# Expert stage in four slots by 32 tokens, with four value gathers and then four key gathers in a row

## The reference, cut to what matters

```
def peer_ffn(xn, w_q, keys1, keys2, u, v):
    q = (xt @ w_q).reshape(n, PEER_HEADS, 2, PEER_HALF)          # 8 heads, 2 x 128
    s1 = einsum('nhd,hkd->nhk', q[:, :, 0], keys1)               # 128 scores
    s2 = einsum('nhd,hkd->nhk', q[:, :, 1], keys2)
    v1, i1 = top_k(s1, 16); v2, i2 = top_k(s2, 16)
    cand = v1[..., :, None] + v2[..., None, :]                   # 256 sums
    top_s, sel = top_k(cand, 16)
    idx = take(i1 * 128 + i2, sel)                               # 16 experts per token and head
    g = softmax(top_s)
    act = gelu(einsum('pd,ped->pe', xb, u[idx]))                 # dot products of 1024
    return einsum('pe,ped->pd', g * act, v[idx])                 # weighted sum of rows of 1024
```

## Time and profile before

| | us |
|---|---|
| median of 3 runs | 4652.41 |
| lowest and highest | 4647.03, 4680.39 |
| span of the profiled execution | 4664.4 |
| expert stage in it, first gather issued to the end | 1476.6 to 4664.4 |

### The profile page before, as it was taken

The page is one execution under the profiler, slowest core; times in us unless marked ns, Lnnn a source line. Parts: engine busy times, 40 slices in busy tenths (PEclk is TensorE's granted clock), DMA queues, the critical chain, the costliest instruction groups (busy, mean ns, idle before and its releaser), DMA issues.

```text
span 4664.4 us, 46976 instructions
## 1 busy us (share of the span) xinstructions
PE 3850.8 (83%) x13480; PEld 2174.6 (47%) x13480; DVE 2478.5 (53%) x6136; ACT 1078.6 (23%) x2482; POOL 2471.3 (53%) x2212
## 2 busy tenths in 40 slices
PE   8999997899884878787887787787788787878787
PEld 7888885555442334343343343343334343434332
DVE  3111004655434666666666666666666666666665
ACT  4221113333210212212222212222222121212221
POOL 0000000000002777777777777777777777777766
PEclk9999997999967999898999898989898999898989
DMA  3222214221136999999999999999999999999988
GB/s 135 89 85 99 77 41 155 75 65 46 53 100 252 369 379 350 385 368 362 368 375 371 367 382 363 360 373 361 358 389 352 363 374 364 346 374 358 361 322 309
DMA packets 393667, 1291.38 MB, mean 277 GB/s; under 512 B 48440, under 2 KB 84536, under 8 KB 391368
## 3 DMA queue, kind: packets, MB, share of 16 engines
q0 software_dynamic: 313920, 1143.22, 65.1%
q1 hardware_dynamic: 61080, 116.93, 7.4%
q10 hardware_dynamic: 18432, 28.42, 1.7%
HBM read 1243.87 MB, written 45.71 MB: 276 GB/s over the span
## 4 chain that ended last, share of the span: by engine, by line
PE 30%; DVE 14%; DMA 12%; issue 8%; POOL 3%; ACT 2%; POOLq 0%; ACTq 0%; DVEq 0%; SPq 0%
PE e_o_ps L1776 24%; DMA e_u_rows<-in_u,e_expert 8%; PE e_q_ps L1744 4%; DMA e_v_rows<-in_v,e_expert 3%; POOL e_v_rows L1429 2%; POOL e_u_rows L1429 1%; DVE e_pairs L1583 1%; DVE e_pairs L1608 1%; DVE e_top_idx L1585 1%; DVE e_top_idx L1582 1%; DVE e_pairs L1612 1%; DVE e_picked L1614 1%; DVE e_top_val L1584 1%; DVE e_pos L1585 1%; PE e_w_ps L1731 1%
## 5 line engine op out<-in xcount | busy, mean ns | idle before, releaser
L1776 PE MATMUL e_o_ps<-e_v_rows,e_diag 128*128 128x512 f32 (+1 forms) x4352 | 2061.4, 626 | 380.7 <-ACT e_diag L1499 289.3
L1631 DVE CUSTOM_DVE_ANT_0 e_u_rows<-e_u_rows,e_xn 128x1024 f32<-128x1024 f32 x1088 | 1300.6, 1223 | 1058.0 <-DMA e_u_rows<-in_u,e_expert 974.5
L1776 PEld LDWEIGHTS e_o_ps<-e_v_rows,e_diag 128*128 128x128 f32 (+1 forms) x4352 | 828.9, 197 | 1464.2 <-issue 1375.3
L1429 POOL DMA_INDIRECT e_v_rows<-in_v,e_expert x1024 | 1177.2, 1150 | 351.1 <-issue 250.8
L1429 POOL DMA_INDIRECT e_u_rows<-in_u,e_expert x1024 | 1114.3, 1088 | 376.4 <-issue 268.7
L1499 ACT ACTIVATE e_diag<-e_ident,e_weight 128x128 f32<-128x128 f32 x1024 | 361.9, 395 | 872.9 <-PE e_o_ps L1776 869.4
L1744 PEld LDWEIGHTS e_q_ps<-e_xnT,e_wq 128*128 128x128 f32 x2304 | 307.7, 209 | 117.9 <-issue 109.2
L1744 PE MATMUL e_q_ps<-e_xnT,e_wq 128*128 128x128 f32 x2304 | 314.4, 294 | 40.3 <-issue 34.0
L578 POOL TENSOR_TENSOR p_gate<-p_gate,gn 128x1024 f32<-128x1024 f32 x8 | 18.9, 2357 | 448.9 <-DMA p_gate<-z_tok 448.9
L373 PE MATMUL j_m<-j_wh,j_xh 128*128 128x512 f32 (+1 forms) x648 | 248.0, 383 | 4.5 <-DVE j_wl L309 2.5
L374 PE MATMUL j_m<-j_wl,j_xh 128*128 128x512 f32 (+1 forms) x648 | 246.2, 380 | 0.0
(11 more groups left out here) (255 smaller groups left out, 3930.1 us busy)
## 6 DMA issues: line engine op xcount, KB each, us to landing
j_w<-in_w_big SPq DMA_DIRECT2D x12, 2048.0 KB, 8.1
z_tok<-j_stage ACTq DMA_DIRECT2D x64, 256.0 KB, 2.0
e_u_rows<-in_u,e_expert POOLq DMA_INDIRECT x1024, 6.3
e_v_rows<-in_v,e_expert POOLq DMA_INDIRECT x1024, 6.3
z_feat<-j_stage ACTq DMA_DIRECT2D x32, 256.0 KB, 2.0
e_wq<-in_wq SPq DMA_DIRECT2D x2, 4096.0 KB, 24.0
e_room<-merged SPq DMA_DIRECT2D x9, 512.0 KB, 6.6
e_h_next<-in_x SPq DMA_DIRECT2D x9, 512.0 KB, 9.3
```

The costliest lines, as they stand in the source:

```text
L1429: pool.indirect_dma_start(ring[:, k % size, :], None, table, bass.IndirectOffsetOnAxis(ap=index[:, h % IDX, k:k + 1], axis=0)).then_inc(go ...
L1631: dve.tensor_tensor_reduce(u_rows[:, k % U_RING, :], u_rows[:, k % U_RING, :], xn[:, :], 1.0, 0.0, ALU.mult, ALU.add, dots[:, h % 2, k:k + ...
L1776: last = pe.matmul(o_ps[0:n, c * BANK:(c + 1) * BANK], diag[:, k % DIAGS, 0:n], v_rows[:, k % V_RING, c * BANK:(c + 1) * BANK], start=Fals ...
```

## The change

The layout of the gathers changes. A gather still fetches 128 rows, one per partition, but now for 32 tokens by 4 slots: partition 32s+i holds token 32j+i and slot 4s+g. For a tile of 128 tokens j and g run over 0 to 3 each, so that there are 16 gathers as before. In detail:

- **Spreading.** Expert numbers and softmax weights now lie side by side in `chosen` (128 x 32), the weights scaled there by 1/sum (`soften`, on DVE, ahead of the next unit's dot products). PE multiplies it with four constant 0/1 matrices (`spreading`), so that every group of 32 partitions gets the 32 tokens of block j; ACT copies eight pieces (`respread`) into `row4` (the gather indices) and `gate4` (the weights in the new order). POOL waits for `row4_ready`. `respread` stands at the head of ACT's loop body, ahead of `norm` and the diagonals, `spreading` at the head of PE's, ahead of the query half.
- **xn in four copies.** `x4` holds for each block j the 32 tokens' xn on all four groups of partitions. SP writes xn to DRAM (`keep_xn`) and reads each block back four times (`load_x4`), 16 loads of 128 KB per tile; the copy `take` on DVE goes.
- **Weighted sum.** The 128x128 diagonals become 128x32 (`stack` scaled by the weights), and block j's matmul writes partitions 32j to 32j+31 of `o_ps`. In a group of four slots the four blocks follow each other for one half of the columns, then for the other. `v_used` counts groups of four, not slots.
- **Order on POOL.** Four value gathers of the unit before, then four key gathers of the unit, four times.
- **Rings.** Six buffers for keys, eight for values as before.
- **Ninth tile.** Two blocks of 32 tokens by 4 slots, 8 gathers of each kind, without the early value gathers and the `pair` copies.
- The constants (identity, ramp, stack, spread) are loaded by SP, 0.3 MB, ahead of the stage's other loads instead of being made on POOL. The loops of the engines are written out in full.

```diff
-    U_RING, V_RING = 8, 8
+    U_RING, V_RING = 6, 8
...
+            def load_x4(t):
+                wait_alone(sp, xn_out, 16 * (t + 1), tick)
+                for j in range(quads(t)):
+                    if t:
+                        wait_alone(sp, u_used, before(t * HEADS - 1) + 4 * (j + 1), tick)
+                    wait_alone(sp, x4_in, 64 * (4 * t + j), tick)
+                    for s in range(4):
+                        sp.dma_start(x4[s * QUAD:(s + 1) * QUAD, j, :],
+                                     xn_dram[t, j * QUAD:(j + 1) * QUAD, :]).then_inc(x4_in, 16)
...
-                    for k in range(TOPK):
-                        if k < slots(t):
-                            u_gather(t, h, k)
-                        if early + k < slots(t, h - 1) and not (isinstance(t, int) and t == 0 and h == 0):
-                            v_gather(t, h - 1, early + k)
+            for unit in range(UNITS):
+                pool.wait_ge(row4_ready, unit + 1)
+                n, ahead = 4 * quads(unit // HEADS), before(unit) - before(unit - 1) if unit else 0
+                for g in range(4):
+                    for k in range(4 * g, min(4 * g + 4, ahead)):
+                        v_gather(unit - 1, k)
+                    for k in range(4 * g, min(4 * g + 4, n)):
+                        u_gather(unit, k)
...
+            def respread(unit):
+                b, n = unit % IDX, quads(unit // HEADS)
+                act.wait_ge(spread_done, unit + 1)
+                wait(act, v_used, 4 * (unit - IDX + 1))
+                for s in range(4):
+                    quad = slice(s * QUAD, (s + 1) * QUAD)
+                    act.activation(gate4[quad, b, 0:4 * n].rearrange("p (g j) -> p j g", j=n),
+                                   spread_ps[quad, 0:n, TOPK + 4 * s:TOPK + 4 * s + 4], ACT.Copy)
+                    last = act.activation(row4[quad, b, 0:4 * n].rearrange("p (g j) -> p j g", j=n),
+                                          spread_ps[quad, 0:n, 4 * s:4 * s + 4], ACT.Copy)
+                last.then_inc(row4_ready, 1)
...
-                for k in range(slots(t, h)):
-                    wait(act, v_used, slots_before(unit) + k - DIAGS + 1)
-                    act.activation(diag[:, k % DIAGS, 0:eye.shape[1]], eye[:, :], ACT.Copy,
-                                   scale=weight[:, h % 2, k:k + 1]).then_inc(diag_ready, 1)
+                n = quads(unit // HEADS)
+                for k in range(4 * n):
+                    if k % n == 0:
+                        wait(act, v_used, 4 * (unit - 1) + k // n + 1)
+                    act.activation(diag[:, k, :], stack[:, :], ACT.Copy,
+                                   scale=weight[:, unit % 2, k:k + 1]).then_inc(diag_ready, 1)
...
+            def soften(unit):
+                b = unit % IDX
+                dve.wait_ge(e_done, unit + 1)
+                chain.link(dve.reciprocal(e_rec[:, b:b + 1], e_sum[:, b:b + 1]))
+                dve.tensor_scalar(chosen[:, b, TOPK:], chosen[:, b, TOPK:], e_rec[:, b:b + 1], None,
+                                  ALU.mult).then_inc(chosen_ready, 1)
...
+            def spreading(unit):
+                pe.wait_ge(chosen_ready, unit + 1)
+                wait(pe, row4_ready, unit)
+                pe.wait_ge(xnT_ready, 2 * (unit // HEADS + 1))
+                for j in range(quads(unit // HEADS)):
+                    last = pe.matmul(spread_ps[:, j, :], spread[:, j, :], chosen[:, unit % IDX, :], start=True, stop=True)
+                last.then_inc(spread_done, 1)
...
+            def v_sum(unit, g):
+                n = quads(unit // HEADS)
+                final = unit % HEADS == HEADS - 1 and g == 3
+                pe.wait_ge(diag_ready, before(unit) + (g + 1) * n)
+                for j in range(n):
+                    seq = before(unit) + g * n + j
+                    pe.wait_ge(v_got[seq % V_RING], 16 * (seq // V_RING + 1))
+                for c in range(D // BANK):
+                    for j in range(n):
+                        last = pe.matmul(o_ps[j * QUAD:(j + 1) * QUAD, c * BANK:(c + 1) * BANK],
+                                         diag[:, g * n + j, :],
+                                         v_rows[:, (before(unit) + g * n + j) % V_RING, c * BANK:(c + 1) * BANK],
+                                         start=False, stop=final)
+                last.then_inc(v_used, 1)
```

More of the change, by code:

```diff
@@ L1339, in peer_stage, with quads, before, group_end @@
         tick = sem("tick")
-        pstep = sem("e_pstep")
         block = ctx.enter_context(nc.Block())
-        LAST = TILES
         def rows(t):
[L1345 to L1361, removed]
+            return NSAMP if t == LAST else P
+        def quads(t):
+            return rows(t) // QUAD
+        def before(unit):
+            return unit * TOPK if unit <= LAST * HEADS else LAST * HEADS * TOPK + (unit - LAST * HEADS) * TOPK // 2
+        def group_end(seq):
+            full = LAST * HEADS * TOPK
+            return (seq // 4 if seq < full else full // 4 + (seq - full) // 2) + 1
         @block.sync
@@ L1392, in _ @@
                     sp.dma_start(keys[:, :, :], keys_dram).then_inc(keys_in, 16)
+            keep_xn(0)
+            load_x4(0)
             sp.dma_start(g_final[:, :], g_final_dram.to_broadcast([P, D])).then_inc(consts, 16)
[L1395 to L1396 removed]
+            for t in range(LAST + 1):
+                if t:
                     store(t - 1)
[L1398 removed]
+                if t < LAST:
                     load_x(t + 1)
                     load_merge(t + 1)
[L1402 to L1405 removed]
+                    keep_xn(t + 1)
+                    load_x4(t + 1)
             store(LAST)
@@ L1456, in _, with u_gather @@
-            tile(0)
-            with pool.Fori(1, LAST) as t:
-                tile(t)
-            tile(LAST)
-            for k in range(slots(LAST)):
-                v_gather(LAST, HEADS - 1, k)
+            def u_gather(unit, q):
+                seq, n = before(unit) + q, quads(unit // HEADS)
+                column = q % 4 * n + q // 4
+                wait_alone(pool, u_used, seq - U_RING + 1, tick)
+                pool.indirect_dma_start(u_rows[:, seq % U_RING, :], None, u_dram,
+                                        bass.IndirectOffsetOnAxis(ap=row4[:, unit % IDX, column:column + 1], axis=0)
+                                        ).then_inc(u_got[seq % U_RING], 16)
@@ L1463, in _ @@
+            for k in range(4 * quads(LAST)):
+                v_gather(UNITS - 1, k)
         @block.scalar
@@ L1653, in out_mean, with weights @@
+            def weights(unit):
+                n = 4 * quads(unit // HEADS)
+                dve.wait_ge(gelu_done, unit + 1)
+                wait(dve, diag_ready, before(unit - 1) if unit else 0)
+                dve.tensor_tensor(weight[:, unit % 2, 0:n], gelus[:, unit % 2, 0:n], gate4[:, unit % IDX, 0:n],
+                                  ALU.mult).then_inc(w_ready, 1)
             def out_mean(t):
```

355 lines of the change are left out of this document (145 added, 210 removed).

## The result

The changed kernel takes 4844 us (median; 4840 to 4860), beside 4662 for the kernel before in the same rounds: ratio 1.039, 95% interval 1.035 to 1.042. It is slower, by the forecast direction and near the forecast size (4800). Its profiled execution spans 4858.1 us against 4664.4, 194 more.

The account below looks back on a forecast made before the run. The prediction took GpSimd's (POOL's) queue as the bound. Waits +158, collisions -20, start +10, end -7 and x4 +10 summed to +151 us: 4815 profiled, 4800 us for the median, range 4565 to 4990.

Parts of the forecast that it names:

- extra cost of head 6: Sixth-numbered head of each tile: the next tile's norm, behind the eight copies, delays the diagonals; POOL waits 10.9 us.
- four column groups side by side: PE's weighted sum: four 32-column outputs run at once, a group of four slots taking 1.7 us at full clock, 3.4 at half.
- The rival that they don't run side by side: PE's weighted sum: a group takes 6.9 us at full clock, +350 us in all, 5150 us; chance 0.14.
- the way to the first group: From selection through soften, spreading, copies, diagonals and query half: the sum's first group ends at S+7.0 to S+10.2.
- S: Time mark in a head: the end of the selection, X+17.0 in the usual head that the forecast read.
- all waits: POOL's added waits over eight tiles, from 1.9 us per usual head, 10.9 in head 6, 4 in head 1: +158 us.
- u6 needs the first dot product ...: nothing: Seventh key gather on POOL: its buffer is free at X+19.2, POOL arrives at X+19.8, so no wait.
- X: Time mark in a head: the start of its last key gather on POOL.
- collisions: POOL's gathers stretched by DVE's dot products, 396 us in the stage: fewer meet while POOL waits, -20 us.
- fewer collisions: Rival: keys issued four in a row lock to dot products, -204 us, mean gather below about 1.05; chance 0.19.
- x4: Writing xn and reading it back, 22 MB by DMA: between 0 and 54 us, mostly hidden, taken as +10 us.
- The first gather: Start of the stage on POOL: first gather at 1491 instead of 1476.6 us, +10 us net of some 5 in collisions.

Follow-up runs that it names:

- b2: The kernel before, with xn held in PSUM, so the dot products read one SBUF and one PSUM tensor: 4466 us, ratio 0.956.
- a5: The changed kernel with spreading behind the sum's first group and the eight copies behind the diagonals, except in head 6 and at the start: 4738 us, ratio 1.014.
- a7: The changed kernel without x4 reloads, with one x4 block for all four, seven key buffers and the late spreading of a5: 4653 us, ratio 0.995.
- a2: The changed kernel with value gather and key gather in turn, one by one: 4878 us, ratio 1.044.
- b1: The kernel before with only POOL's order changed, four value gathers, then four key gathers: 4711 us, ratio 1.007.

## Why the prediction was right or wrong

**Right: what bounds the stage.** 1033 us of PE work saved bought no time, shorter gathers did (b2), and so did opening the gates at which POOL waits (a5, a7). The forecast named the direction, the place (ninth value gather, "<-PE") and an extra cost of head 6, and all three are there. Head 6 was to cost 10.9 us, all at the ninth value gather; it costs 13, of which only 4.1 are there and the rest at the seventh key gather.

**Right: four column groups side by side.** A group of four slots takes 1.92 us at full clock (a5's and a7's units), 3.64 at half, 2.74 where the clock rises inside it. The estimate was 1.7 and 3.4, 0.2 short at each. The rival that they don't run side by side is dead.

**Right in its steps, small in its price: the way to the first group.** Forecast to end at S+7.0 to S+10.2, it ends at S+9.4, with the query half at half clock (3.76) in it as said. The copies took 1.06 us and not 2.0, the spreading 1.92. But I let the wait end with the group: POOL's next gather begins 0.8 us after the group's end (2036.60 to 2037.44). So v8, the ninth value gather, waits 2.9 us on average in a usual head (1.5 to 3.7) instead of 1.9. Even so, the waits for values (217 us) are about what the sum had for all waits (158, and the 52 of the kernel before).

**Wrong: "u6 needs the first dot product ...: nothing".** This is the step that failed. It compared X+19.2, the end of the first dot product, with X+19.8, POOL's arrival at u6, the seventh key gather. Over the usual heads of the full tiles the first is X+20.3 on average and the second X+19.3 (in the unit above X+20.6 and X+20.0). The forecast had read 7.2 us to the selection off one unit, where 7.5 was already the average of the kernel before and the changed one has 7.9; and with fewer collisions POOL comes sooner. The same 0.8 us lie between the dot product's end (2029.28) and POOL's gather (2030.09). The order in fours is not the cause: with the gathers in turn (a2) the seventh key gather waits even longer, 214 us instead of 181. The wait is mostly 1 to 2.4 us in usual heads. In head 6 it is 7.7 to 8.9 and in the first head of a tile 4 to 5, and these two the comparison did not look at. Together it is 190 us with the ninth tile, in a place priced at nothing. That is the larger part of why the waits rose by 342 and not by 168. A margin of 0.6 us between two sums of some 19 us each was no margin.

**Wrong: collisions.** The sum had -20, by the time POOL stands still; -169 came. The mechanism was written down as the rival "fewer collisions", at -204 for a mean gather under 1.05, and it is 1.044. b1 shows 130 of it with no other change; with the gathers in turn (a2) the changed kernel still has 51 fewer than the kernel before, twice the 25 of the sum. So I weighted as two outcomes what were two independent terms: the waits rose and the collisions fell, in the same run.

**Two errors that offset each other.** Waits 174 us too low and collisions 144 too high (and start and end 12 too low) leave +193 beside +151. The forecast was near for that reason and not because its terms were right; by its own test ("I am wrong if POOL's mean gather moves by more than 0.05 us either way") it was wrong, since the mean moved by 0.078. That the sum came near was luck.

**Small terms.** x4 cost 41 us by the medians and not 10, within the bounds of 0 to 54: it was priced by the DMA's mean room, but it collides at a tile's end, where the last keys are what POOL's gate hangs on. The first gather came 21 us later, not 15. The end gained 1 us, not 7: the last sum isn't limited by PE but by diagonals and landings, and runs at the half clock. Last sums of the changed kernel, PE in order of time:

```profile
4838.47 5.01 PE L1756 MATMUL e_o_ps<-e_v_rows,e_diag 128*32 128x512 f32 x16 [5.23 <-ACT e_diag L1500]
...
4847.34 1.91 PE L1756 MATMUL e_o_ps<-e_v_rows,e_diag 128*32 128x512 f32 x8 [0.59 <-DMA e_v_rows<-in_v,e_row]
```

**Open.** Head 6 still costs POOL 13 us per tile in the changed kernel, and no version tried moves the norm ahead of the eight copies. Why the order in fours saves as many collisions as it does was not taken apart: that gathers and dot products fall into step is argued from the single rows, and only the sum is measured. The changed layout with one operand of the dot product in PSUM, which would show it free of collisions, was not tried.

## What to carry to other kernels

When the busy time of one issuing queue and its fixed pauses add up to the stage, a faster engine elsewhere buys nothing, and a longer way to one of that queue's gates costs what it takes beyond the slack; write down the margin of every gate, in the odd heads too and with the wake-up time of the waiter, and call a margin under 1 us a wait. Gates in a row on one queue hand time to each other: here opening the first alone gained nothing, the second alone three quarters of what both gave. So test them singly and together. And look at what lengthens the queue's own instructions before anything else: here a change of one operand from SBUF to PSUM was worth more than the whole layout.

## What the runs showed of the hardware that I had not expected

- A gather on GpSimd that begins during the dot product on DVE, with two SBUF inputs, ends 0.81 us after it and takes up to 1.97 us; with one of the inputs in PSUM it takes 0.94 all the same, and DVE is no slower (1218 against 1223 ns). The Trainium skill (GPSIMD Engine Reference, Key points) says that the two engines meet in SBUF for such instructions; the trace agrees, and the busy time that it cost GpSimd in this kernel was 370 us of 4664.
- Four 32-column outputs at four partition offsets run side by side to 3.7 times the speed (7.03 us to 1.92 us for a group of four slots).
- With PE's load down from 80% to 44%, its mean granted clock fell from 0.90 to 0.67, so part of the gain of a faster sum went back where a group came right after a pause (1.92 becomes 3.64).
- POOL resumed some 0.8 us after the end of the work that released it, at both of its gates. 0.3 of that is the pause that every gather has; the other 0.5, at 131 waits, are an estimated 65 us of the 407.
- While POOL issued without a break the DMA moved 410 GB/s (b2, 2220 to 2280 us), where 512 KB each 1.25 us are 419. Without the collisions, POOL and the DMA are limits of nearly the same size.
